# A reordered middle, reordered rotations, and a first output product in four pieces

## The chip, the cores and the metric

One core of a Trainium2 chip runs the whole program in one launch. The metric is the device time in microseconds. The kernel before took 2297.06, 2299.01 and 2300.14 us in three runs, median 2299.01.

## The reference

Two blocks in float32 on 1024 tokens of width 1024. The first is a mixer and a squared-ReLU MLP, the second an attention with compressed queries and keys (MLA):

```
h = rmsnorm(x, ln_mlp_g);  x = x + square(relu(h @ w_mlp_up)) @ w_mlp_down    # width 4096
h = x @ w_in_2;  x_q, x_kv, k_rope_raw, gate_a, u_pool, gate_b = split(h)
q  = rms_norm(x_q) @ w_uq          # 4 heads of 128 + 64 rotated
kv = rms_norm(x_kv) @ w_ukv        # keys and values, 4 heads of 128
s = (q_nope @ k_nope + rope(q_rope) @ rope(k_rope)) * scale, causal;  o = softmax(s) @ v
y = concat(o * silu(gate_a), pool_branch(u_pool) * silu(gate_b)) @ w_out_2
out = layer_norm(alpha * x + y)
```

## The kernel before

All large products are made in three passes of TensorE from operands that are split into a high and a low part (hi x hi, hi x lo, lo x hi). ScalarE copies the high part, VectorE (activations) or GpSimd (weights) subtracts it for the low part.

**The MLP's steps.** Two-by-two block products are made by Winograd's seven products P1 to P7. Steps 0 to 15 multiply up, steps 16 to 31 down, steps 32 to 40 (the strip) are the second block's input projection. The list RUN holds (step, product) in the order of TensorE; in steps 1 to 31 it is P1 P5 P6 P2 P7 P3 P4. A run's number is its index: step 16 begins at run 112, step 17 at 119, step 18 at 126. run() of TensorE (L1558 to L1588) waits for the weight's low part (wt_ok, GpSimd L1196), for its banks (evicted) and for its operand's low part (t_ok), and issues 12 matmuls (L1585). P1, P6, P7 and P4 of a step add up in one pair of banks, P5 and P3 in another, P2 has a third; after each run VectorE's event() adds the banks into xB (L2951), and the next run in those banks waits for it.

**Weights.** SP loads a step's weight blocks as wraw (load_pair, L915). GpSimd makes the sums S1 to S4 (L1152 to L1168); ScalarE's weight_hi (L2205) copies the high part of each weight at the turn W_TURN; GpSimd subtracts (L1196). After run 117's weight GpSimd also makes hsum, the last sums of the hidden blocks (L1180 to L1185).

**Split operands of the down steps.** 56 pieces j, one for each product of two steps, come from staged loads. ScalarE's split_hi(j) (L2275) stands at turn T_TURN[j] of its loop, behind that turn's weight_hi; VectorE's split_lo(j) (L2983) stands behind event(T_TURN[j]). T_TURN is 1 apart for j up to 6, then 2 apart: 117, 119, 121, 123 for j=7 to 10, and so on to 213 for j=55. Piece j is first used in step 16 + 2(j // 7), by the product P1, P5, P6, P2, P7, P3 or P4 as j % 7 is 0 to 6. So j=13 (turn 129) is used by run 132, j=20 (143) by run 146, and so on.

**SP in the middle.** At run 113 two loads of xB from x_d (1 MB each, L972 and L973) are issued, then staged loads; load_pair(st + 2) comes at the step's fourth run. Each waits in SP's one queue. event() of steps 16 and 17's P1 waits for those loads (x_in).

**Into the strip.** final_lo (L3033) splits the last results. The strip's operands T1 to T4 are differences of blocks of xB: t_sum (VectorE L3050, four operations each), t_his (ScalarE L2288), t_los (VectorE L3057). VectorE then evicts the strip by add_strip (L3121), ScalarE by copy_strip (L2295).

**Late strip and rotations.** ScalarE's root(xkv) (L1883, L1885), the reciprocal root of the compressed keys' mean square, stands ahead of step 40's copies. Then come the units uq (query heads) and ukv (keys, values): ScalarE copies each one's high part (q2st L2427, k L2436, V2h L2441), VectorE's low2 (L3242) the low part, which frees the bank. rope(r) (L3248 to L3250) rotates qr and kr with `turned`, which SP fills from kr and qr; rope_hi and rope_lo (L3258) split the result; the parts are parked in HBM and come back as q2S.

**The attention.** 32 items i, in pairs. TensorE issues logits2(i+2), turn2(i) (eight transposes, L1756), values2 (L1769). VectorE: least (L3299), normalise2 (L3307), turned_lo (L3312), gated (L3319). Behind them half_product (L1800) makes 16 units of the output product from actC, whose parts are split by branch_half (ScalarE) and low (VectorE L2528).

Of the kernel before, what the change touches and what calls it, by code (L numbers as in the profile page):

```python
# [18 lines left out]
ALU = mybir.AluOpType  # L19
# [195 lines left out]
RUN += [(st, p) for st in range(1, STEPS) for p in ("P1", "P5", "P6", "P2", "P7", "P3", "P4")]  # L215
# [12 lines left out]
for _st, _p in RUN:  # L228
    if WEIGHT[_p][0] == "S":
        SUM_NO[_st, _p] = len(SUM_NO) + 1  # L230
# [4 lines left out]
T_RING, STAGED = 10, 8  # L235

# [53 lines left out]
def split_turns():  # L290

    turn, room = [], []
    for j in range(N_SPLIT):
# [6 lines left out]
        turn.append(max(r, turn[-1] + (2 if j >= 7 else 1)) if turn else r + 2)  # L300
# [46 lines left out]
def build(nc, t):  # L347

    with ExitStack() as ctx:
# [395 lines left out]
        def product_bank(c):  # L745

            n = FIRST["out2"] + c
            col = (c // 2) % 2 * HALF
            return pair[n % 2][:, col:col + HALF]
# [68 lines left out]
        def _(sp):  # L818
# [148 lines left out]
            for at_run in range(7 * N_PAIR, N_ALL):  # L967
                if at_run == 7 * N_PAIR + 1:
# [4 lines left out]
                    sp.dma_start(xB[:, 1:4:2, :], x_d[:, 1:4:2, :]).then_inc(x_in, 16)  # L973
                st, p = RUN[at_run - 1]
# [3 lines left out]
                if at_run == START[st] + 3 and st + 2 < ALL_STEPS:  # L978
                    load_pair(st + 2)
# [79 lines left out]
        def _(pool):  # L1059
# [112 lines left out]

            def last_unit_sums():
# [13 lines left out]
            for i, (st, p) in enumerate(RUN):  # L1187
                if p in ("P1", "Q1"):
                    pool.wait_ge(pair_in[st % 2], 16 * (st // 2 + 1))
                if i + 1 < N_ALL and WEIGHT[RUN[i + 1][1]][0] == "S":  # L1190
                    weight_sum(i + 1)
                pool.wait_ge(wt_hi, i + 1)
# [40 lines left out]
        def _(pe):  # L1233
# [539 lines left out]

            pe.wait_ge(r_hi, 3)
# [3 lines left out]
            for i in range(N2 + 2):  # L1778
                if i + 2 < N2:
                    logits2(i + 2)  # L1780
                if i < N2:
                    turn2(i)
                if i >= 2:
                    values2((i - 2) // 2, i % 2)

            def half_product(j, half):
# [6 lines left out]
                if c == 1:  # L1793
                    pe.wait_ge(branch_ok, N2_GROUP)
                for k in range(NT):
                    if j == 0:
                        pe.wait_ge(lo_ok, base + 6 + half * NT + k + 1)
# [22 lines left out]
            for half in range(2):  # L1820
                half_product(0, half)
# [27 lines left out]
        def _(act):  # L1849
# [433 lines left out]
            def t_his(name):  # L2283

                c = ("T1", "T2", "T4", "T3").index(name)
                act.wait_ge(tsum_ok, T_SUMS + (16 if name == "T4" else 4 * c + 4))
# [20 lines left out]
            for at_run in range(2, N_RUN):  # L2307
# [5 lines left out]
                if at_run == 7:  # L2313
                    for p in ("P2", "P7", "P3", "P4"):
                        square_out(NO[0, p])
                late = START[N_PAIR + 1]
# [7 lines left out]
                for j in range(N_SPLIT):  # L2324
                    if T_TURN[j] == at_run:
# [36 lines left out]
            for i in range(START[STEPS + 1], N_ALL):  # L2362
# [31 lines left out]
                if i == NO[STEPS + 7, "P4"]:  # L2394
                    root(("stat", "xkv"), (squares_used, STAT_BASE["xq"] + 2), EPSV, rstd_kv[:, :])
                if i == NO[STEPS + 8, "P6"]:
# [7 lines left out]
            for r in range(2):  # L2404
                read_unit(n, n % 2, n // 2, qr[:, r, :], ACT.Copy)
                n += 1
                if r == 0:
                    act.wait_ge(lo_ok, base + 6)
# [14 lines left out]
            for h in range(4):  # L2423
# [7 lines left out]
                if h < 3:  # L2431
                    rope_hi(h)
# [12 lines left out]
            def branch_half(half, tiles):  # L2445
                if tiles[-1] > 3:
                    act.wait_ge(gb_moved, 32)
# [16 lines left out]
            for i in range(N2):  # L2464
# [3 lines left out]
                if i == N2 - 2:  # L2468
                    branch_half(0, range(3))
# [1124 lines left out]
```

## Time and profile before

| | |
|---|---|
| profiled execution, its span | 2299.54 us, 2297.7 us |
| TensorE (PE) busy | 2235.4 us, 97% |
| VectorE (DVE) busy | 1694.5 us, 74% |
| GpSimd (POOL) busy | 1195.4 us, 52% |
| ScalarE (ACT) busy | 837.3 us, 36% |
| TensorE's mean granted clock, as a share of full speed | 0.995 |

The matmuls of a row overlap: a run's 12 follow each other every 0.227 us, though each one's own time is 0.39. A bracket at a row's end is the engine's idle time before it and what released it.

### The profile page before, as it was taken

The numbers are of one execution on the slowest core, as the hardware profiler recorded it, in microseconds if no ns is written. First come the engines' busy times: TensorE is split into PE (matmuls) and PEld (weight loads), VectorE is DVE, ScalarE is ACT, GpSimd is POOL, SyncE is SP. The second block draws the span as 40 slices with busy tenths as digits, with TensorE's granted clock in tenths as the row PEclk, the third lists the DMA queues.
The fourth block names the chain that finished last, engine by engine and source line by source line (L and its number), as shares of the span: only waits on it lengthen the run. The fifth ranks groups of instructions, "written<-read, shape, count | busy, mean of one in ns | idle before, by whom it ended". The sixth has DMA issues, their size and how long they took to land. (4 is left out here: it accounts for less than half of the span.)

```text
span 2297.7 us, 29211 instructions
## 1 busy us (share of the span) xinstructions
PE 2235.4 (97%) x10722; PEld 1849.6 (80%) x10722; DVE 1694.5 (74%) x2037; ACT 837.3 (36%) x1165; POOL 1195.4 (52%) x895
## 2 busy tenths in 40 slices
PE   7999999999999999999999999899999999999998
PEld 5678888888888899787878888788888777778886
DVE  7899999986778354446587766677777866578777
ACT  4312243123334256213343333444343434344423
POOL 4136553333323266334478988998886678400140
PEclk9999999999999999999999999999999999999999
DMA  4121123633332422444234445654442212441231
GB/s 155 37 83 64 64 92 106 169 138 113 108 128 92 129 66 65 156 146 165 83 135 153 151 171 189 256 193 156 147 156 101 70 37 92 131 152 49 65 110 73
DMA packets 93733, 272.50 MB, mean 119 GB/s; under 512 B 8800, under 2 KB 25320, under 8 KB 87080
## 3 DMA queue, kind: packets, MB, share of 16 engines
q1 hardware_dynamic: 76544, 206.86, 26.8%
q10 hardware_dynamic: 17064, 63.99, 7.9%
q8 instruction: 77, 1.26, 0.2%
q14 instruction: 48, 0.39, 0.1%
HBM read 186.13 MB, written 83.90 MB: 118 GB/s over the span
## 5 line engine op out<-in xcount | busy, mean ns | idle before, releaser
L1247 PE MATMUL pair<-actA,w_hi 128*128 128x512 f32 x2016 | 624.5, 391 | 2.1 <-issue 2.1
L1247 PEld LDWEIGHTS pair<-actA,w_hi 128*128 128x128 f32 x2016 | 377.5, 188 | 81.4 <-ACT sq L1938 2.9
L1247 PE MATMUL pair<-actA,w_lo 128*128 128x512 f32 x1008 | 393.1, 390 | 0.0
L1066 POOL TENSOR_TENSOR pad<-pad 128x1 f32<-128x1 f32 x93 | 24.7, 266 | 585.3 <-PE pair L1247 506.4
L1585 PE MATMUL pair<-tring,wsp 128*128 128x512 f32 x1344 | 307.4, 391 | 8.1 <-issue 7.1
L1585 PEld LDWEIGHTS pair<-tring,wsp 128*128 128x128 f32 x1344 | 253.2, 189 | 62.2 <-issue 9.0
L1196 POOL TENSOR_TENSOR wsp<-wraw,wsp 128x512 fp32r<-128x512 f32 x124 | 188.8, 1523 | 75.5 <-ACT wsp L2205 75.1
L1247 PEld LDWEIGHTS pair<-actA,w_lo 128*128 128x128 f32 x1008 | 189.5, 188 | 39.8
L1070 POOL TENSOR_TENSOR w_lo<-raw,w_hi 128x1024 fp32r<-128x1024 f32 (+1 forms) x93 | 209.1, 2248 | 7.5
L1585 PE MATMUL pair<-tsp,wsp 128*128 128x512 f32 x768 | 184.2, 391 | 4.4 <-DVE tsp L2910 2.1
L2951 DVE TENSOR_TENSOR xB<-pair,xB 128x1024 f32<-128x1024 f32 x112 | 136.3, 1219 | 70.3 <-PE pair L1585 70.1
L2638 DVE MAX8 top<-pen 128x8 f32<-128x384 f32 (+5 forms) x192 | 171.7, 894 | 6.4
L1585 PEld LDWEIGHTS pair<-tsp,wsp 128*128 128x128 f32 x768 | 143.5, 188 | 37.5 <-DVE tsp L2910 4.3
L2640 DVE MATCH_REPLACE8 pen<-top,pen 128x384 f32<-128x384 f32 (+5 forms) x192 | 168.2, 876 | 0.0
L1585 PE MATMUL pair<-bsp,wsp 128*128 128x512 f32 x576 | 138.4, 389 | 0.0
L2205 ACT CAST wsp<-wraw 128x512 fp32r<-128x512 f32 x124 | 77.0, 621 | 160.4 <-PE pair L1585 140.2
L1196 POOL TENSOR_TENSOR wsp<-wsum_a,wsp 128x512 fp32r<-128x512 f32 x80 | 127.7, 1596 | 9.0 <-ACT wsp L2205 9.0
L1585 PEld LDWEIGHTS pair<-bsp,wsp 128*128 128x128 f32 x576 | 108.1, 188 | 22.5
L1922 ACT ACTIVATE stage<-pair 128x1024 f32<-128x1024 f32 x40 | 41.0, 1026 | 228.1 <-PE pair L1247 228.1
L1610 PE MATMUL pair<-bin,wsp 128*128 128x512 f32 x456 | 109.2, 393 | 3.4 <-ACT u L2295 2.1
L2983 DVE TENSOR_TENSOR tring<-staged,tring 128x1024 fp32r<-128x1024 f32 x56 | 97.7, 1744 | 13.9 <-ACT tring L2275 13.9
L1610 PEld LDWEIGHTS pair<-bin,wsp 128*128 128x128 f32 x456 | 86.6, 190 | 22.2 <-issue 4.2
(454 smaller groups left out, 4530.2 us busy)
## 6 DMA issues: line engine op xcount, KB each, us to landing
wraw<-w_pair SPq DMA_DIRECT2D x41, 1024.0 KB, 6.0
raw<-w_in SPq DMA_DIRECT2D x62, 512.0 KB, 3.5
staged<-hid_d SPq DMA_DIRECT2D x56, 512.0 KB, 3.3
proj<-stage ACTq DMA_DIRECT2D x40, 512.0 KB, 2.6
hid_d<-hsum SPq DMA_DIRECT2D x16, 1024.0 KB, 5.0
gates<-proj ACTq DMA_DIRECT2D x18, 512.0 KB, 5.2
raw<-w_out SPq DMA_DIRECT2D x16, 512.0 KB, 3.5
hid_d<-hid SPq DMA_DIRECT2D x16, 512.0 KB, 2.8
```

Source lines behind the costliest of these rows:

```text
L1066: nc.gpsimd.tensor_tensor(pad[:, 0:1], pad[:, 1:2], pad[:, 1:2], ALU.add)
L1070: nc.gpsimd.tensor_tensor(w_lo[:, par, 0:w], raw[:, par, 0:w], w_hi[:, par, 0:w].bitcast(F32), ALU.subtract).then_inc(w_split, 1)
L1196: nc.gpsimd.tensor_tensor(dst[:, 1, :], src, dst[:, 0, :].bitcast(F32), ALU.subtract).then_inc(wt_ok, 1)
L1247: last = nc.tensor.matmul(pair[par][:, cols], w[:, slot, wk], x[:, cols], start=(k == 0 and i == 0), stop=(k == kt - 1 and i == 2))
L1585: mm = nc.tensor.matmul(out, w[:, wp, wk], x[:, xp, k, :], start=(fresh and k == 0 and m == 0), stop=(k == ks - 1 and m == 2), skip_group_ ...
L1610: mm = nc.tensor.matmul(out, w[:, wp, wk], x(xp, k), start=(first and k == 0 and m == 0), stop=(last and k == 3 and m == 2), skip_group_ch ...
L1922: nc.scalar.activation(dst, pair[par][:, :], func).then_inc(unit_out[par], 1)
L2205: nc.scalar.copy(wsp[W_SLOT[i]][:, 0, :], src).then_inc(wt_hi, 1)
L2638: V.max(top8[:, :], sc).then_inc(topk, 1)
L2640: V.match_replace(sc, top8[:, :], sc, PICKED).then_inc(topk, 1)
L2951: V.tensor_tensor(acc, src.rearrange("p (s n) -> p s n", n=HALF), acc, ALU.add).then_inc(evicted, 1)
L2983: V.tensor_tensor(dst[:, 1, :, :].rearrange("p k n -> p (k n)"), staged[:, j % STAGED, :], dst[:, 0, :, :].rearrange("p k n -> p (k n)").b ...
```

## The change

Five places, each on several engines.

- Step 17's order becomes P1 P5 P2 P6 P7 P3 P4. T_TURN[8] becomes 121 (it was 119), T_TURN[9] 122 (121), and each later j's turn is one run later. ScalarE issues split_hi(6) and (7) at run 115, ahead of that turn's other copies. SP issues load_pair(18) right behind the two loads of xB and then waits for these before the staged loads.
- T3's four sums move from VectorE to GpSimd (third_sum, ahead of the weight of the first run of step 33). On VectorE T1's sums stand behind final_lo and T2's ahead of t_los("T1").
- root(xkv) moves behind step 40's P6 copy; norm2 of xkv moves behind the low parts of xq. The rotations' operations are spread otherwise between the units, and the load of cs waits for no low part any more.
- The first unit of the output product, half_product(0, 0), becomes first_product: four pieces of six matmuls at items 30 and 31, between the last two values and after the loop. It writes to the bank of item 30's logits. Its inputs are split one tile an item (VectorE, items 25 to 30) or two (ScalarE, items 24, 26, 28, 30).
- The product's second unit waits for the gated group 15 and the fourth for group 16, where the second waited for 16.

```diff
 RUN = [(0, p) for p in ("P1", "P5", "P2", "P6", "P3", "P7", "P4")]
-RUN += [(st, p) for st in range(1, STEPS) for p in ("P1", "P5", "P6", "P2", "P7", "P3", "P4")]
+RUN += [(st, p) for st in range(1, N_PAIR + 1) for p in ("P1", "P5", "P6", "P2", "P7", "P3", "P4")]
+RUN += [(N_PAIR + 1, p) for p in ("P1", "P5", "P2", "P6", "P7", "P3", "P4")]
+RUN += [(st, p) for st in range(N_PAIR + 2, STEPS) for p in ("P1", "P5", "P6", "P2", "P7", "P3", "P4")]
...
     if WEIGHT[_p][0] == "S":
-        SUM_NO[_st, _p] = len(SUM_NO) + 1
+        SUM_NO[_st, _p] = len(SUM_NO) + 1 + 4 * (NO[_st, _p] > NO[STEPS + 1, "P5"])
...
 T_RING, STAGED = 10, 8
+FIRST_HALF = [0, 4, 1, 5, 2, 6, 3, 7]
...
         room.append(r)
-        turn.append(max(r, turn[-1] + (2 if j >= 7 else 1)) if turn else r + 2)
+        if j == 8:
+            r = max(r, NO[N_PAIR + 1, "P2"])
+        turn.append(max(r, turn[-1] + (2 if j >= 7 and j != 9 else 1)) if turn else r + 2)
...
             col = (c // 2) % 2 * HALF
+            if c == 0:
+                return mpair(("qk", 1, N2 - 2))[:, 0:HALF]
...
                     sp.dma_start(xB[:, 1:4:2, :], x_d[:, 1:4:2, :]).then_inc(x_in, 16)
+                    load_pair(N_PAIR + 2)
+                    sp.wait_ge(x_in, 16 * (NT + 6))
...
                 st = RUN[at_run][0]
-                if at_run == START[st] + 3 and st + 2 < ALL_STEPS:
+                if at_run == START[st] + 3 and N_PAIR < st < ALL_STEPS - 2:
...
+            def third_sum():
+
+                pool.wait_ge(tsum_ok, T_SUMS + 4)
+                pool.wait_ge(lo_ok, 4 * NT + 4)
+                for k in range(4):
+                    nc.gpsimd.tensor_tensor(xB[:, k, HALF:S], xB[:, 4 + k, HALF:S], xB[:, k, HALF:S],
+                                            ALU.subtract).then_inc(summed, 1)
+                sums[0] += 4
...
                     weight_sum(i + 1)
+                if i == START[STEPS + 1]:
+                    third_sum()
...
+            def first_product(part):
+                n, out = FIRST["out2"], product_bank(0)
+                whi, wlo = kept(0)
+                if part == 0:
+                    pe.wait_ge(w_split, n + 1)
+                    wait_done(pe, ("qk", 1, N2 - 2))
+                for s in (2 * part, 2 * part + 1):
+                    k = FIRST_HALF[s]
+                    pe.wait_ge(lo_ok, base + 6 + s + 1)
+                    wk, xh, xl = slice(k * P, (k + 1) * P), actC[:, 0, k, 0, :], actC[:, 0, k, 1, :]
+                    for i, (w, x) in enumerate(((whi, xh), (whi, xl), (wlo, xh))):
+                        mm = nc.tensor.matmul(out, w[:, wk], x, start=(s == 0 and i == 0),
+                                              stop=(s == NT - 1 and i == 2))
+                if part == 3:
+                    mm.then_inc(unit_mm, 1)
...
                     logits2(i + 2)
+                if N2 - 2 <= i <= N2:
+                    first_product(i - N2 + 2)
...
                     values2((i - 2) // 2, i % 2)
+            first_product(3)
...
                 if c == 1:
+                    pe.wait_ge(branch_ok, N2_GROUP - 1)
+                if c == 3:
...
                     if j == 0:
-                        pe.wait_ge(lo_ok, base + 6 + half * NT + k + 1)
+                        pe.wait_ge(lo_ok, base + 6 + NT + k + 1)
...
             for half in range(2):
-                half_product(0, half)
+                if half:
+                    half_product(0, half)
...
-                c = ("T1", "T2", "T4", "T3").index(name)
-                act.wait_ge(tsum_ok, T_SUMS + (16 if name == "T4" else 4 * c + 4))
+                if name == "T3":
+                    act.wait_ge(summed, SUM_NO[STEPS + 1, "P5"] + 4)
+                else:
+                    act.wait_ge(tsum_ok, T_SUMS + 4 * ("T1", "T2", "T4").index(name) + 4)
...
                         square_out(NO[0, p])
+                if at_run == NO[N_PAIR, "P2"]:
+                    split_hi(6)
+                    split_hi(7)
...
                 for j in range(N_SPLIT):
-                    if T_TURN[j] == at_run:
+                    if T_TURN[j] == at_run and j not in (6, 7):
...
                     root(("stat", "xq"), (squares_used, STAT_BASE["xq"] + 1), EPSV, rstd_q[:, :])
-                if i == NO[STEPS + 7, "P4"]:
+                if i == NO[STEPS + 8, "P6"]:
                     root(("stat", "xkv"), (squares_used, STAT_BASE["xq"] + 2), EPSV, rstd_kv[:, :])
-                if i == NO[STEPS + 8, "P6"]:
...
                 if r == 0:
-                    act.wait_ge(lo_ok, base + 6)
...
                     park_q2(h - 1)
-                if h < 3:
-                    rope_hi(h)
+                if h != 1:
+                    rope_hi(max(h - 1, 0))
...
             def branch_half(half, tiles):
-                if tiles[-1] > 3:
-                    act.wait_ge(gb_moved, 32)
+                act.wait_ge(gb_moved, 32)
...
                 turned_hi(i)
-                if i == N2 - 2:
-                    branch_half(0, range(3))
-            branch_half(0, range(3, NT))
+                if i % 2 == 0 and i >= N2 - 8:
+                    s = i - N2 + 8
+                    branch_half(0, FIRST_HALF[s:s + 2])
...
-                c = ("T1", "T2", "T4", "T3").index(name)
+                c = ("T1", "T2", "T4").index(name)
...
                     b11, b12_, b21, b22 = xB[:, k, 0:HALF], xB[:, k, HALF:S], xB[:, 4 + k, 0:HALF], xB[:, 4 + k, HALF:S]
-                    x, y = {"T1": (b12_, b11), "T2": (b22, b11), "T3": (b22, b12_), "T4": (b21, t2f[:, k, :])}[name]
+                    x, y = {"T1": (b12_, b11), "T2": (b22, b11), "T4": (b21, t2f[:, k, :])}[name]
...
                     final_lo(("P5", "P6", "P7", "P3").index(p))
-                if st == STEPS - 1 and p == "P7":
-                    t_sum("T1", (0, 1))
-            t_sum("T1", (2, 3))
+            t_sum("T1", (0, 1))
...
                 final_lo(c)
+            t_sum("T1", (2, 3))
+            t_sum("T2")
             t_los("T1")
-            t_sum("T2")
...
             t_los("T2")
-            t_sum("T3")
...
             norm2([(g, xq[:, g, :]) for g in range(1, 4)], "q_norm_2", rstd_q)
-            dve.wait_ge(rstd_ok, 13)
-            norm2([(g, xkv[:, g, :]) for g in range(2)], "kv_norm_2", rstd_kv)
...
                 low(base + g, xq_lo[:, g, :], xq[:, g, :], xq_hi[:, g, :])
+            dve.wait_ge(rstd_ok, 13)
+            norm2([(g, xkv[:, g, :]) for g in range(2)], "kv_norm_2", rstd_kv)
...
                 low2(n, q2_hi, h + 1, q2st[:, h % 2, 1, :], q2st[:, h % 2, 0, :]).then_inc(unit_out[n % 2], 1)
-                if h < 2:
-                    rope(h)
-                for k in ((), (), (0,), (1, 2))[h]:
-                    rope_lo(k)
+                if h == 0:
+                    rope_lo(0)
+                elif h == 1:
+                    rope(0)
+                elif h == 2:
+                    rope(1)
+                    rope_lo(1)
...
                 low2(n, kv_hi, h + 1, k2[:, 1, h, :], k2[:, 0, h, :]).then_inc(unit_out[n % 2], 1)
+                if h == 0:
+                    rope_lo(2)
...
+
+            def first_low(s):
+                j = FIRST_HALF[s]
+                low(base + s, actC[:, 0, j, 1, :], branch(j, 0), actC[:, 0, j, 0, :])
...
                     gated(i // 2 - 2)
-                if i == N2 - 2:
-                    low_half(0, range(3))
-            low_half(0, range(3, 6))
+                if N2 - 7 <= i < N2 - 1:
+                    first_low(i - N2 + 7)
             gated(N2_GROUP - 2)
-            low_half(0, range(6, NT))
+            first_low(6)
+            first_low(7)
```

## Rows read from the trace of the kernel before

**Rows 1.** The page: busy time of TensorE and its weight loads.
```profile
PE 2235.4 (97%) x10722; PEld 1849.6 (80%) x10722; DVE 1694.5 (74%) x2037; ACT 837.3 (36%) x1165; POOL 1195.4 (52%) x895
```

**Rows 2.** Waits of TensorE from 1440 us on: total, times, longest, all in us.
```profile
PE pair L1247 <- DVE q2st L3242: 2.6, 2, 1.4
...
PE pair L1756 <- DVE PTl L3312: 2.3, 2, 1.2
...
PE pair L1247 <- DVE k L3242: 1.8, 1, 1.8
PE pair L1610 <- DVE bin L3033: 1.3, 1, 1.3
PE pair L1769 <- DVE PTl L3312: 0.9, 1, 0.9
```

**Rows 3.** Timeline of TensorE, 1486 to 1503: start, length, instruction, count.
```profile
1494.37 7.28 PE L1585 MATMUL pair<-tring,wsp 128*128 128x512 f32 x24 [6.87 <-issue]
1501.84 1.39 PE L1585 MATMUL pair<-tring,wsp 128*128 128x512 f32 x5 [0.19 <-issue]
```

**Rows 4.** Timeline of VectorE, 1466 to 1503.
```profile
1490.16 1.84 DVE L2983 TENSOR_TENSOR tring<-staged,tring 128x1024 fp32r<-128x1024 f32 x1 [9.56 <-ACT tring L2275]
1491.93 2.34 DVE L2951 TENSOR_TENSOR xB<-pair,xB 128x1024 f32<-128x1024 f32 x2
```

**Rows 5.** Timeline of ScalarE, 1466 to 1503.
```profile
1489.09 1.04 ACT L2275 CAST tring<-staged 128x1024 fp32r<-128x1024 f32 x1
```

**Rows 6.** Timeline of GpSimd, 1466 to 1503.
```profile
1490.88 2.25 POOL L1196 TENSOR_TENSOR wsp<-wraw,wsp 128x512 fp32r<-128x512 f32 x1
1495.86 1.28 POOL L1152 TENSOR_TENSOR wsum_a<-wraw 128x512 f32<-128x512 f32 x1 [2.73 <-DMA wraw<-w_pair]
```

**Rows 7.** Timelines of VectorE in the down steps, 1557 to 1565 and 1580 to 1585.
```profile
1560.39 1.24 DVE L2983 TENSOR_TENSOR tring<-staged,tring 128x1024 fp32r<-128x1024 f32 x1
...
1581.01 1.23 DVE L2951 TENSOR_TENSOR xB<-pair,xB 128x1024 f32<-128x1024 f32 x1 [1.24 <-PE pair L1585]
1582.15 1.93 DVE L2983 TENSOR_TENSOR tring<-staged,tring 128x1024 fp32r<-128x1024 f32 x1
```

**Rows 8.** Timeline of TensorE, 1580 to 1585: two runs without a stall.
```profile
1579.67 5.60 PE L1585 MATMUL pair<-tring,wsp 128*128 128x512 f32 x24
```

**Rows 9.** Timeline of GpSimd, 1578.5 to 1585.
```profile
1581.71 1.29 POOL L1196 TENSOR_TENSOR wsp<-wsum_c,wsp 128x512 fp32r<-128x512 f32 x1 [0.66 <-ACT wsp L2205]
```

**Rows 10.** Timelines of VectorE, GpSimd and TensorE into the strip, 1775 to 1825.
```profile
1789.13 2.49 DVE L3050 TENSOR_TENSOR t2f<-xB 128x512 f32<-128x512 f32 x4
...
1795.91 6.48 DVE L3057 TENSOR_TENSOR bin<-t2f,bin 128x512 fp32r<-128x512 f32 x4 [0.60 <-ACT bin L2288]
1802.31 6.87 DVE L3050 TENSOR_TENSOR xB<-xB 128x512 f32<-128x512 f32 x4
1809.88 8.50 DVE L3057 TENSOR_TENSOR tA<-xB,tA 128x512 fp32r<-128x512 f32 x8 [0.69 <-ACT tA L2288]
...
1792.71 1.45 POOL L1196 TENSOR_TENSOR wsp<-wraw,wsp 128x512 fp32r<-128x512 f32 x1 [11.64 <-ACT wsp L2205]
...
1819.08 3.00 PE L1610 MATMUL pair<-tA,wsp 128*128 128x512 f32 x12 [2.04 <-issue]
```

**Rows 11.** Timeline of TensorE late in the strip, 1947 to 2046.
```profile
1955.12 7.27 PE L1610 MATMUL pair<-bin,wsp 128*128 128x512 f32 x24 [2.09 <-ACT u L2295]
```

**Rows 12.** Stretches: length, busy PE, PEld, DVE, ACT, POOL (instructions), PE clock, DMA, GB/s.
```profile
1468.00:1487.50 19.50, 19.32 (x84) 15.69 (x84) 11.51 (x10) 5.31 (x8) 19.42 (x14) 1.00 0.46 171
...
1955.07:1958.48 3.41, 3.36 (x8) 2.71 (x9) 2.96 (x2) 1.42 (x3) 2.92 (x2) 0.50 0.01 2
```

**Rows 13.** Stretches of the key units, with the same columns.
```profile
2020.00:2026.00 6.00, 5.22 (x23) 4.35 (x24) 2.90 (x3) 1.06 (x2) 0.00 (x0) 1.00 1.01 351
```

**Rows 14.** Timeline of TensorE, 2020 to 2050: the first logits.
```profile
2037.73 0.47 PE L1741 MATMUL pair<-k,q2S 128*128 128x512 f32 x1 [0.28 <-issue]
```

**Rows 15.** Timeline of VectorE in the last items, 2155 to 2205.
```profile
2165.09 1.40 DVE L3307 TENSOR_SCALAR L<-L,tiny 128x1024 f32<-128x1024 f32 x1
```

## Prediction

> **What bounds the kernel now.** First the page's line of busy times: TensorE works 2235.4 of 2297.7 us [rows 1], so the end is set by PE, and a reordering can win only PE's idle time, 62.3 us in all, or time in which PE ran at its lower clock. Then PE's waits over the last 850 us and the stretches around each: a 6.87 us stall in the middle [rows 3], 1.3 where the last down step passes into the strip, 2.09 late in the strip [rows 11], 2.6 and 1.8 in the rotations, 2.3 and 0.9 at the end of the attention [rows 2]. These are the places that the change touches. The reader is to ask at each: which instruction ended the wait, what stood ahead of it in its own queue, and what is next to be late. Last, the steady rhythm of the down steps [rows 7, 8], which loses nothing now and whose order the change also shifts.
>
> The profiled execution took 2299.54 us (span 2297.7 and 1.84 around it). The sum is made against that; the median of the timed runs is 2299.01, 0.5 less. A measurement here can tell about 0.2% (4.6 us) from no change.
>
> **A1, the middle.** Run 121 (step 17's third) starts at 1494.37 after 6.87 of idling [rows 3]. It needed two evictions of DVE, which ended at 1494.27; in DVE's queue they stood behind split_lo(7), which sat from 1480.6 to 1490.16 for ScalarE's split_hi(7) [rows 4]; that copy began at 1489.09 [rows 5], behind five weight copies that wait for GpSimd's sums. The change issues split_hi(6) and (7) ahead of those copies, so this block goes, and run 121 becomes a P2, whose bank pair is another. Runs 121 and 122 then end at 1487.34 + 24 x 0.227 = 1492.8. (A run is 12 matmuls at 0.227, or 2.72; a row of 24 matmuls shows 5.60 with the last one's own length in it [rows 8].)
>
> What is late next? Run 123 (P7) now follows P6 directly in one bank pair and needs P6's eviction. On DVE that eviction stands behind split_lo(8), moved from turn 119 to 121. split_lo(8) waits for split_hi(8), and in ScalarE's queue that stands at turn 121 behind weight_hi(128), the copy of step 18's S2. GpSimd makes that sum only after the weight splits of step 17, of which the last ends at 1493.13 [rows 6]. Before, GpSimd then idled 2.73 for wraw(18) [rows 6]; the load is moved forward, right behind the two xB reloads, so this idling goes. Sum S1, a split and sum S2 at 1.28 each (as the first sum there) end at 1497.0; split_hi's 1.04 [rows 5] and the copy ahead of it, half as wide, some 0.6: 1498.7; split_lo 1.9 [rows 4]: 1500.6; eviction 1.17 (2.34 for two): 1501.8. Run 123 starts at about 1501.9; before, it started at 1501.84 [rows 3]. The stall is moved from in front of run 121 to in front of run 123. Behind the stall of 6.87 the next 24 matmuls took 7.28 for 5.60 [rows 3, 8], as behind the one late in the strip, where the granted clock was 0.50, the 1.2 GHz level, for 3.4 us [rows 12]. That comes again, now behind run 123: +1.7 at most. I take **+1.5**, bounds 0 and +3.5 (the second adds staged loads that now wait for x). If split_lo(8) holds nothing up, only P6's eviction itself lies between the runs, about 1.4: run 123 at 1494.2, or **-7.6**.
>
> **A2, the turn of every later split.** From j=9 each split_lo comes one run later. For most it is needed 4 to 9 runs after its turn. But the split of the P4 quarter in each even step (j=13, 20, ... 55, seven of them) had 3 runs and now has 2. j=20 runs alone, 1.24, at 1560.39 [rows 7]; with one run more it lands where the odd steps have a split now, as j=24: PE's run releases the eviction at 1581.01 (0.20 after its end, by the starts of its matmuls), the split takes 1582.15 to 1584.08 [rows 7], 1.93 instead of 1.24 because GpSimd's weight split of 1581.71 [rows 9] overlaps it. So it ends 3.07 + 0.20 = 3.27 after the run's end, and PE needs it 2.72 after: 0.55 late, 0.15 for the semaphore, some 0.08 to restart: 0.78 x 7 = **+5.3** (bounds: 0 if it runs in 1.24, ending 2.58 after; +7 at 1.0 each, if GpSimd begins its 1.29 just ahead of it).
>
> **B, into the strip.** T1's first sums no longer stand ahead of final_lo(4), so the 1.30 wait goes [rows 2]. T3's four sums, 6.87 on DVE, go to GpSimd, idle for 11.64 there [rows 10]. But GpSimd's four sums now meet DVE's: four DVE operations of this shape took 2.49 while GpSimd was idle, and 6.48 beside it [rows 10]. T2's sums and T1's low parts, 2.49 each, now cost up to 6.5 each, the GpSimd weight work starts a microsecond later, and T2's low parts end near 1812 rather than 1802.4. T4's low parts end at 1820 to 1822 against 1818.4, and P4 waits for the addition behind them, as before at 1819.08 [rows 10]. I take **+2.5**, bounds -1.7 (no clash) and +3.8.
>
> The row shows DVE at 1.62 an operation beside GpSimd. The Trainium skill (SBUF — State Buffer, "SBUF: two separate sides") says that whichever of the two starts first holds the shared ports for its whole instruction, and Perfetto Trace Analysis ("Optimizing Scalar/DVE Operations") that work moved between these two engines might not help. The trace agrees as to the blocking. By the rule in full GpSimd's four sums would hold the ports 4 x 1.28 = 5.1 us where DVE's held them 2.5, and B would be about +2.6, an estimate.
>
> **C, the end of the strip and the rotations.** root(xkv), two activations with a table load each, moves on ScalarE behind (40,P6); the strip copy it held up comes in time. It cost 2.09 of stall, and the 24 matmuls behind it took 7.27 for 5.60 [rows 8, 11] at the low clock [rows 12]: with 0.15 to restart -3.9. Of the rotations' stalls, the first (1.2, on the landing of turned) stays, since its whole chain moves along; the second (1.4) and that of the third key unit (1.8) go [rows 2], and one of some 0.5 is new (by the lengths of the same instructions in their new order), at the second key unit behind rope(1) and its low part. That would be -6.5. But logits2(0) waits for q2S, issued into a stretch in which the DMA engines are full [rows 13] and whose first transfer moves only with the 3.9 and not with the two stalls. So PE arrives earlier and waits there: before it waited 0.28 [rows 14]. **-3.3**, bounds -2.2 (a stall at the value units halves the clock for a while, as here at 1955: 1.7) and -6.5 (q2S in time).
>
> **D, the last items.** At the end of the items PE lost 2.3 and 0.9 to the transposed low parts [rows 2]. The first product's 24 matmuls come in between in four pieces of 6 (1.36 us each) and no longer behind: the 3.2 of idling go, with 0.15 of restart at each of the three, -3.65 at best. In exchange DVE gets one more low part (0.6) in each of six items, and beside GpSimd's split of w_out a DVE operation of 0.75 elsewhere took 1.40 [rows 15]; one such can push the next transposes by 0.6 and, with a low part in between, up to 1.75. The bank, GpSimd's later splits and the loads are free in time. **-2.5**, bounds -1.9 and -3.65.
>
> **Sum**: 1.5 + 5.3 + 2.5 - 3.3 - 2.5 = +3.5: 2303.0 by the profiled execution, **2302.5** against the median: no change that can be told, a shade slower. Its own range is 2298 to 2307.
>
> **Rivals.**
> 1. *The middle's stall goes.* For it: the only thing that holds P6's eviction is a split that is first used six runs on, and GpSimd could be ahead of my sum, if wraw(18) is there by 1488 and its operations run at 1.28. Against it: GpSimd is busy 19.42 of the 19.50 us up to the stall [rows 12] and cannot start step 18 before 1493.1. A1 is then -7.6: 3.5 - 9.1 = -5.6, 2293.4.
> 2. *Slower: DVE and GpSimd take turns at full price.* Place: the seven shifted splits, the strip's start and the last six items; price: A2 +6.5, B +3.8, D -1.9, so 1.5 + 6.5 + 3.8 - 3.3 - 1.9 = +6.6, 2305.6. It decides where each DVE operation begins after GpSimd's, not before. For it: the odd steps' 1.93 repeats all the way through; against: off the path it costs nothing, as in every odd step now.
> 3. *The shifted splits cost nothing.* If DVE begins ahead of GpSimd each time (as at 1560.39), A2 is 0: -1.8, 2297.2. Against it: it is the odd steps' own pattern that the even ones take over.
> 4. *The change does not fill the tail*, D = 0, as the pieces wait for their low parts: +6, 2305; small.
>
> **How the numbers follow.** Forecast 0.45, rival 1 0.20, rival 2 0.18, rival 3 0.12, rival 4 0.05. Faster by over 0.2% (below 2294.4): most of rival 1 and a part of rival 3 with rival 1's gain, 0.22. Slower by over 0.2% (above 2303.6): rivals 2 and 4 and a quarter of the forecast, 0.34. Between: 0.44. The range takes in rival 1 with a larger C below (2291) and rival 2 with A1's far end above (2309).
>
> **What would show it.** A1: run 121 without a stall, and an idle of 8 to 9 us ahead of run 123 with split_lo(8) at about 1499 on DVE. A2: seven PE waits of 0.5 to 0.9 on DVE's tring, 38.1 us apart. B: DVE's T2 sums at 1.6 to 1.7 each. C: no wait on u at 1953, 24 matmuls in 5.44, and a longer wait ahead of the first logits. D: transposes of the last items that follow without a gap. The prediction fails if run 123 starts by 1495, if DVE's splits stay at 1.24 in those seven places, or if the wait at the first logits doesn't appear.

## Result and profile after

The changed kernel takes 2322.06 us in the median of four runs (2317.85 to 2323.35) against 2299.57 for the kernel before in four runs: a ratio of 1.0088, 95% interval [1.0072, 1.0104], slower by 0.9%. I had forecast 2302.5 and a range up to 2309. The profiled execution's span is 2320.2 against 2297.7. TensorE works hardly longer (2235.4 before, [rows 1]); the page of the changed kernel begins with its busy time, share and count:

```profile
PE 2241.8 (97%) x10722; PEld 1852.1 (80%) x10722; DVE 1704.1 (73%) x2033; ACT 838.2 (36%) x1165; POOL 1198.6 (52%) x899
```

Cut at the same matmuls in both traces, the difference stands where the prediction's terms are (us, from the starts of TensorE's first matmuls in the two profiled executions):

| stretch | before | after | differs | forecast |
|---|---|---|---|---|
| run 119 to run 130 (A1) | 39.07 | 45.61 | +6.5 | +1.5 |
| run 130 to the strip (A2) | 255.68 | 260.47 | +4.8 | +5.3 |
| the strip's first 16 products (B) | 47.99 | 51.27 | +3.3 | +2.5 |
| the rest of the strip (C, first part) | 145.75 | 141.82 | -3.9 | -3.9 |
| last input unit to the first logits (C, rest) | 67.34 | 69.41 | +2.1 | +0.6 |
| first logits to item 24 | 104.96 | 104.86 | -0.1 | 0 |
| item 24 to the end (D) | 154.99 | 165.12 | +10.1 | -2.5 |

TensorE's waits of the changed kernel from 1440 us on, with total, times and longest, answer to [rows 2]:

```profile
PE pair L1605 <- issue: 13.6, 1, 13.6
PE pair L1847 <- DVE xB L3411: 9.1, 1, 9.1
PE pair L1267 <- DVE q2st L3284: 5.4, 1, 5.4
PE pair L1605 <- DVE tring L3027: 4.0, 7, 0.7
PE pair L1630 <- DVE bin L3101: 2.6, 2, 2.2
PE pair L1776 <- DVE PTl L3359: 2.1, 3, 1.8
```

The larger waits of before at the places of the change are gone, and larger ones stand in their stead. The first two are the surprise. In the middle, the timelines of the changed kernel's TensorE, VectorE and GpSimd answer to [rows 3, 4, 6]:

```profile
1506.32 26.54 PE L1605 MATMUL pair<-tring,wsp 128*128 128x512 f32 x108 [13.63 <-issue]
...
1498.35 6.73 DVE L3027 TENSOR_TENSOR tring<-staged,tring 128x1024 fp32r<-128x1024 f32 x1 [6.71 <-ACT tring L2317]
1505.00 1.21 DVE L2995 TENSOR_TENSOR xB<-pair,xB 128x1024 f32<-128x1024 f32 x1
...
1497.84 1.27 POOL L1216 TENSOR_TENSOR wsp<-wsum_b,wsp 128x512 fp32r<-128x512 f32 x1
1499.06 1.27 POOL L1170 TENSOR_TENSOR wsum_a<-wraw 128x512 f32<-128x512 f32 x1
1500.29 1.27 POOL L1216 TENSOR_TENSOR wsp<-wraw,wsp 128x512 fp32r<-128x512 f32 x1
1501.51 1.27 POOL L1177 TENSOR_TENSOR wsum_c<-wraw,wsum_b 128x512 f32<-128x512 f32 x1
1502.72 1.27 POOL L1216 TENSOR_TENSOR wsp<-wsum_a,wsp 128x512 fp32r<-128x512 f32 x1
```

Run 123 waits, as forecast, for the eviction behind split_lo(8), and split_lo(8) starts at 1498.35 where I had 1498.7. But it takes 6.73 us for work of 1.2. It ends at 1505.08, 1.09 behind the last of five GpSimd operations in a row, four of which began after it and none of which was lengthened. In the changed kernel's end, VectorE, GpSimd and TensorE:

```profile
2206.95 6.39 DVE L2572 TENSOR_TENSOR actC<-u,actC 128x512 fp32r<-128x512 f32 x4 [0.76 <-ACT actC L1934]
2213.26 7.61 DVE L2572 TENSOR_TENSOR actC<-gb,actC 128x512 fp32r<-128x512 f32 x4
2220.91 1.41 DVE L3411 SCALAR_TENSOR_TENSOR xB<-xB,pair 128x512 f32<-128x512 f32 x2
...
2207.26 1.29 POOL L1247 CAST w_kept<-raw 128x1024 fp32r<-128x1024 f32 x1 [22.14 <-PE pair L1805]
2208.62 2.73 POOL L1249 TENSOR_TENSOR w_kept<-raw,w_kept 128x1024 fp32r<-128x1024 f32 x1
...
2221.65 2.07 PE L1847 MATMUL pair<-xB,cst 128*128 128x512 f32 x2 [9.10 <-DVE xB L3411]
```

The first product now ends as the values end, so GpSimd's third weight split (released by TensorE's L1805 at 2207.26) begins just when VectorE begins the eight low parts of half 1. These take 14.0 us where the kernel before took 5.0, and the operation that the first mean waits for (L3411) stands behind them.

### The profile page after: what moved, and what is told of

Same layout as the page of the kernel before. It is cut to its first block and busy times, and to the rows that moved or that the text cites. A ratio compares the mean times of both kernels' runs of the same rounds, so it can differ in the third digit from the quotient of the medians.

```text
span 2320.2 us, 29212 instructions
## 1 busy us (share of the span) xinstructions
PE 2241.8 (97%) x10722; PEld 1852.1 (80%) x10722; DVE 1704.1 (73%) x2033; ACT 838.2 (36%) x1165; POOL 1198.6 (52%) x899
## 5 line engine op out<-in xcount | busy, mean ns | idle before, releaser
L1605 PEld LDWEIGHTS pair<-bsp,wsp 128*128 128x128 f32 x576 | 108.1, 188 | 22.5
```

Source lines behind the costliest of these rows:

```text
L1605: mm = nc.tensor.matmul(out, w[:, wp, wk], x[:, xp, k, :], start=(fresh and k == 0 and m == 0), stop=(k == ks - 1 and m == 2), skip_group_ ...
```

## Experiments

Ratios are to the kernel before on the same chip, with their 95% intervals. Stretches are those of the table, each from one profiled execution. Runs of one kernel spread by 3 to 20 us, so a difference of 2 us between two experiments is read from the stretches and not from the whole times.

**1. The first product's result taken out first.**

```diff
             dve.wait_ge(branch_ok, N2_GROUP)
-            low_half(1, range(NT))
...
+            move(0)
+            low_half(1, range(NT))
             dve.wait_ge(lo_ok, base + 2 * NT)
...
-                move(c)
+                if half:
+                    move(c)
```


> The changed kernel with one edit at the end: VectorE takes the first product's result out (move(0)) ahead of the eight low parts of half 1, not behind them. Theory (the 9.10 us wait ahead of the first mean is VectorE's queue: move(0) stands behind eight low parts that take 14.0 us instead of 5.0, because GpSimd's weight splits, which the earlier first product releases earlier, now fall on them): the low parts still take 12 to 14 us, but the wait ahead of the first mean falls under 1 us and the run is 8 to 9.5 us faster than the changed kernel, about 2313. Rival (the pieces of the first product or the borrowed bank hold the mean up): the wait stays at 9 and the time at 2322.

Measured: 2310.90 us, 1.0055 [1.0037, 1.0073]. The stretch from item 24 on fell from 165.12 to 153.90. The low parts still took 13.2 us, but nothing waits for them; of the end's waits two of 1.8 and 0.4 are left, beside one of 0.7 that the kernel before has too. The theory holds; it gave two us more than the wait, as the matmuls behind it no longer run slowly (in the changed kernel 25 of them had taken 7.62, at a granted clock of 0.72, where 25 at 0.227 take 5.7).

**2. GpSimd's third split waits for the low parts.**

```diff
                 if j == 2:
                     pool.wait_ge(unit_mm, FIRST["out2"] + 1)
-                if j == 6:
                     pool.wait_ge(lo_ok, 4 * NT + 10 + 2 * NT)
```


> The changed kernel with one edit at the end: GpSimd's third weight split of the output product waits until VectorE's sixteen low parts are done. Theory (shared SBUF access of VectorE and GpSimd): the eight low parts of half 1 fall from 14.0 to about 5.0 us, the wait ahead of the first mean from 9.10 to under 1.5; the third unit's weights come some 3 us late, so 5 to 8 us faster than the changed kernel, 2314 to 2317. Rival (the low parts are slow for a reason of their own, as their place in SBUF or the copies beside them): they stay at 12 to 14 us and nothing is won.

Measured: 2313.57 us, 1.0068 [1.005, 1.0085]. VectorE in this kernel:

```profile
2204.50 2.50 DVE L2571 TENSOR_TENSOR actC<-u,actC 128x512 fp32r<-128x512 f32 x4 [0.76 <-ACT actC L1933]
2206.91 2.49 DVE L2571 TENSOR_TENSOR actC<-gb,actC 128x512 fp32r<-128x512 f32 x4
```

The same eight operations take 5.0 us when GpSimd holds still: it is GpSimd's work that makes them 14. The 9.10 went and 1.77 for the later weights came. The theory holds. The run is 8.5 us faster than the changed kernel, half a us more than expected. It also showed that the middle has two outcomes. Its code there is that of the changed kernel, and its VectorE:

```profile
1499.64 1.85 DVE L3026 TENSOR_TENSOR tring<-staged,tring 128x1024 fp32r<-128x1024 f32 x1 [7.02 <-ACT tring L2316]
1501.42 1.21 DVE L2994 TENSOR_TENSOR xB<-pair,xB 128x1024 f32<-128x1024 f32 x1
```

Here GpSimd let it in after one operation, and the stall is 8.77. Run 123 starts at 1502.73, 19.8 behind run 119; forecast were 1501.9 and 20.0. In four of the five profiles with this middle (the changed kernel, 1, 5 and 6) it was 13.63 or 13.64.

**3. GpSimd pauses in the middle until split_lo(8) is done.**

```diff
+                if i == NO[N_PAIR + 2, "P6"]:
+                    pool.wait_ge(t_ok, 16 + 9)
                 if i + 1 < N_ALL and WEIGHT[RUN[i + 1][1]][0] == "S":
```


> The changed kernel with one edit in the middle: GpSimd makes the sum S2's successors of step 18 (from the weight of its P6 on) only when split_lo(8) is done. Theory (split_lo(8) took 6.73 us instead of 1.2 to 1.9 because five GpSimd operations in a row went ahead of it): it falls to 1.2 to 2.6 us, run 123 starts 4 to 5.5 us earlier, at about 1502, the stall ahead of it is about 9 us, and the run is 4 to 5 us faster than the changed kernel, about 2317.5. Rival (the length of split_lo(8) has another cause, as the staged loads that land beside it): 6 to 7 us as before, run 123 at 1506.

Measured: 2315.42 us, 1.0073 [1.0055, 1.009]. VectorE and GpSimd of this kernel:

```profile
1497.82 1.23 DVE L3029 TENSOR_TENSOR tring<-staged,tring 128x1024 fp32r<-128x1024 f32 x1 [6.89 <-ACT tring L2319]
...
1499.13 1.27 POOL L1218 TENSOR_TENSOR wsp<-wsum_b,wsp 128x512 fp32r<-128x512 f32 x1 [1.77 <-DVE tring L3029]
```

The theory holds: split_lo(8) takes 1.23 and the stall falls to 8.14, so 5.5 us of the 13.63 are GpSimd's operations that went ahead. The rest is the order, in which split_lo(8) still waits 6.89 for its high part.

**4. The turns of before.**

```diff
-        if j == 8:
-            r = max(r, NO[N_PAIR + 1, "P2"])
-        turn.append(max(r, turn[-1] + (2 if j >= 7 and j != 9 else 1)) if turn else r + 2)
+        turn.append(max(r, turn[-1] + (2 if j >= 7 else 1)) if turn else r + 2)
```


> The changed kernel with the turns of the splits (T_TURN) as they were before; step 17's order and all else stay. Theory: split_lo(8) no longer stands ahead of run 122's eviction, so run 123 starts at 1495 to 1498 instead of 1506.3, and the six waits of 0.54 in the even steps go: 11 to 15 us faster than the changed kernel, 2307 to 2311. Rival (it is GpSimd's unbroken work that holds VectorE's splits, wherever they stand): the six waits go (3.7 us), but split_lo(8), now ahead of run 120's eviction, is held to 1500 or later and the stall only moves: 3 to 6 us faster, 2316 to 2319.

Measured: 2316.49 us, 1.0075 [1.0056, 1.0094]. Run 130 to the strip takes 255.68, to the hundredth that of before: the later turns cost 4.8, as forecast. But run 123 starts at 1502.65 still. VectorE:

```profile
1494.87 1.89 DVE L3025 TENSOR_TENSOR tring<-staged,tring 128x1024 fp32r<-128x1024 f32 x1 [5.50 <-ACT tring L2315]
1496.68 2.34 DVE L2993 TENSOR_TENSOR xB<-pair,xB 128x1024 f32<-128x1024 f32 x2
1499.57 1.85 DVE L3025 TENSOR_TENSOR tring<-staged,tring 128x1024 fp32r<-128x1024 f32 x1 [0.55 <-ACT tring L2315]
1501.34 1.21 DVE L2993 TENSOR_TENSOR xB<-pair,xB 128x1024 f32<-128x1024 f32 x1
```

The time is the rival's, and so is the stall that only moves, but not the place: split_lo(8) is through by 1496.8, and now split_lo(9) at its turn 121 stands ahead of run 122's eviction, behind a high part that waits for the same sum of GpSimd. The 11 to 15 us of the theory come only when every split leaves the way (experiment 7).

**5. T3's sums back on VectorE**, on top of experiment 1.

```diff
             t_sum("T1", (2, 3))
             t_sum("T2")
             t_los("T1")
             t_sum("T4")
             t_los("T2")
+            t_sum("T3")
             t_los("T3")
...
-                if i == START[STEPS + 1]:
-                    third_sum()
```


> The first experiment's kernel (the first product's result taken out ahead of half 1's low parts) with T3's four sums back on VectorE, behind t_los(T2) as before; T1's and T2's sums stay where the change put them. Theory (GpSimd's four sums cost more in VectorE's other sums, which go from 0.6 to 1.7 each, than they take from it): T2's sums fall from 6.9 to about 2.5 us, the wait of 2.2 us at T2's low parts and the 3 us of slow matmuls behind it go; a wait of 0 to 2 at T4's low parts comes back; 2 to 5 us faster than the first experiment. Rival (VectorE's 2.4 to 6.9 us saved count): T4's low parts come late again, the stretch is as long or 1 to 2 us longer.

Measured: 2310.98 us, 1.0056 [1.0039, 1.0072]; the strip's first products take 51.52 against 51.22 in experiment 1. The rival holds. T2's sums fell to 2.50, and the wait only moved, to T4's low parts (TensorE of this kernel):

```profile
1830.83 4.35 PE L1619 MATMUL pair<-tA,wsp 128*128 128x512 f32 x11 [5.24 <-issue]
```

So T3's place alone gives nothing back. With the order of T1's and T2's sums undone as well the stretch is 47.99, 49.59 and 49.56 (experiments 9 to 11). T3 on GpSimd with the old order of the sums was not run.

**6. The rotations' order of before**, on top of experiment 1.

```diff
-                if h == 0:
-                    rope_lo(0)
-                elif h == 1:
-                    rope(0)
-                elif h == 2:
-                    rope(1)
-                    rope_lo(1)
+                if h < 2:
+                    rope(h)
+                for k in ((), (), (0,), (1, 2))[h]:
+                    rope_lo(k)
```
(and rope_hi in ScalarE's loop)

> The first experiment's kernel with the rotations' order on VectorE and ScalarE as before; root(xkv) stays behind step 40's P6 and the load of cs still waits for no low part. Theory (in the changed order ScalarE's copy of the third query head waits for a parked one to land in HBM, 6.5 us of idling, and its successor follows late): the 4 to 5 us wait at the second key unit becomes waits of 1.2, 1.4 and 1.8, and the stretch from the first query unit to the first logits falls by 1 to 3 us against the first experiment. Rival (the stretch is set by the DMA engines, whichever order): the first logits come as late, within 0.5 us.

Measured: 2308.94 us, 1.0044 [1.0028, 1.0061]. The last input unit to the first logits: 63.95 against 67.74, and against 67.34 in the kernel before. The waits of 1.2 and 1.4 did not come back, only that of 1.73: 3.8 us, more than expected, and the rival fails.

**7. The middle's splits behind the evictions**, on top of experiment 1: split_lo(8), (9), (10) at turns 122, 123, 124, the later ones at those of before.

```diff
+                if at_run in (119, 120, 121):
+                    split_hi(at_run - 111)
                 late = START[N_PAIR + 1]
...
-                    load_pair(N_PAIR + 2)
-                    sp.wait_ge(x_in, 16 * (NT + 6))
```


> The first experiment's kernel with the middle ordered so that no split stands ahead of an eviction that step 17 needs: split_lo(8), (9), (10) behind runs 122, 123, 124 and every later one at its turn of before, their high parts on ScalarE ahead of the weight copies at runs 119 to 121, and load_pair(18) back behind the staged loads. Theory (run 123 is held by P6's eviction alone once the splits are out of VectorE's way): the stall ahead of run 123 falls from 9 to 14 us to 1.3 to 3, the slow clock behind it goes, the six waits of 0.54 go: 12 to 17 us faster than the first experiment, 2294 to 2299. Rival (GpSimd's unbroken work holds VectorE wherever the splits stand): waits of together 6 to 10 us come up in the runs 124 to 131 instead, and 4 to 8 us are won.

Measured: 2297.75 us, 0.9995 [0.9985, 1.0005], 13.2 faster than experiment 1, in the theory's range. The stall ahead of run 123 is 1.36, but a new one of 4.75 came five runs later (TensorE, VectorE of this kernel):

```profile
1494.05 13.88 PE L1603 MATMUL pair<-tring,wsp 128*128 128x512 f32 x60 [1.36 <-issue]
1512.69 7.53 PE L1603 MATMUL pair<-tring,wsp 128*128 128x512 f32 x25 [4.75 <-POOL wsp L1214]
...
1510.12 1.33 DVE L3027 TENSOR_TENSOR tring<-staged,tring 128x1024 fp32r<-128x1024 f32 x1 [5.96 <-ACT tring L2315]
1511.37 2.34 DVE L2995 TENSOR_TENSOR xB<-pair,xB 128x1024 f32<-128x1024 f32 x2
```

The label says GpSimd; but run 128's weight was split by 1504.2 in this trace, and the eviction of run 126, behind split_lo(11), ended at 1512.6. Experiment 9 tests this.

**8. All parts together**: 7, 5, 6 and 1.

> All of these together: step 17's new order with its splits out of the way, T3's sums on VectorE, the rotations' old order, root(xkv) moved, and the first product in four pieces with its result taken out ahead of half 1's low parts. If the parts add: the first experiment less 12 to 17, less 2 to 5, less 1 to 3, so 2287 to 2296, and faster than the kernel before by 3 to 11 us. If the sum is set by other waits in its stead (the rivals of the three): 2299 to 2304.

Measured: 2294.86 us, 0.9982 [0.9973, 0.9992]: 2287 to 2296 holds, though 5 gave nothing.

**9. The high parts of splits 8 to 13 ahead of the weight copies, the load early, the strip as before.**

```diff
-                if at_run in (119, 120, 121):
+                if at_run in range(119, 125):
                     split_hi(at_run - 111)
...
+                    load_pair(N_PAIR + 2)
...
-            t_sum("T1", (2, 3))
-            t_sum("T2")
             t_los("T1")
+            t_sum("T2")
```
(T1's first two sums too stand where they stood before)

> The kernel of all parts together with three edits: the high parts of splits 8 to 13 all stand ahead of ScalarE's weight copies (runs 119 to 124), where 8 to 10 did; load_pair(18) stands right behind the two loads of xB again; and the way into the strip is as in the kernel before (T3 on VectorE, T2's sums behind T1's low parts). Theory (the 5 us wait that came up ahead of run 128 is split_lo(11), which waits for its high part behind a weight copy that waits for GpSimd, and holds run 126's eviction): it goes, and from the start of run 119 to that of run 130 it takes 31.5 to 34 us instead of 38.6; the strip's first five steps take 48.0 instead of 51.7; in all 2284 to 2288, 11 to 15 us faster than the kernel before. Rival (GpSimd itself is late with the weights of step 18, as the profile's label at that wait says): with the load earlier 2 to 3 us of the 5 go, 35.5 to 37 for the eleven runs, in all 2288 to 2291.

Measured: 2288.00 us, 0.9956 [0.9941, 0.9971]: faster than both kernels. From run 119 to run 130 it takes 31.54, the strip's first products 47.99, and no wait is left between run 123 and run 135 (TensorE):

```profile
1493.93 32.90 PE L1593 MATMUL pair<-tring,wsp 128*128 128x512 f32 x144 [1.36 <-issue]
1528.56 1.62 PE L1593 MATMUL pair<-tring,wsp 128*128 128x512 f32 x6 [1.72 <-issue]
```

The rival had 35.5 to 37 for the first. So it was VectorE's queue and not GpSimd's lateness, although the load came earlier in the same run: in experiment 7's trace the weight had been there 8.5 us before the wait ended. Run 130 to the strip takes 257.69, 2.0 more than before, with the 1.72 ahead of run 135 in it.

**10. The load of cs waits again**, on top of 9.

```diff
                 if r == 0:
+                    act.wait_ge(lo_ok, base + 6)
                     act.wait_ge(cs_gb0_moved, 32)
```


> The kernel of the run before this one with one edit: the load of cs waits for the sixth low part again, as in the kernel before. Theory (of the rotations the change's only gain is this earlier load: the first rotation no longer waits for it, nor the transfers that stood beside it): from the end of the strip's last units to the first logits it takes 67 to 67.5 us instead of 63.9, 3 to 3.5 us slower than the run before. Rival (the gain comes from the later normalisation of xkv or from what lies around it): 64 to 65, no difference that can be told.

Measured: 2292.51 us, 0.9981 [0.9964, 0.9998]. The last input unit to the first logits: 67.02 against 63.94. The theory holds by this stretch, and the waits of the rotations (2.6 in two, 1.8) are those of before again. By the whole times alone it could not be told: twelve runs from 2286 to 2303, and an interval that meets experiment 9's.

**11. The end as before**, on top of 9 without its pieces.

```diff
-                if N2 - 2 <= i <= N2:
-                    first_product(i - N2 + 2)
...
-            first_product(3)
...
             for half in range(2):
-                if half:
-                    half_product(0, half)
+                half_product(0, half)
```
(and the low parts, high parts and bank of the first product as before)

> The ninth experiment's kernel with the end of the attention and the first unit of the output product as in the kernel before (no pieces, no early low parts; half_product(0, 0) behind the values). Theory (with GpSimd's splits falling on VectorE's low parts the pieces win 3 us of waits and lose 1.5 to 2.2 at a transpose behind a slowed normalisation, so they are worth 1 us or less): from the 24th item on 154.5 to 155.5 us where the pieces took 153.6 to 156.1 in five profiles; the time within 1.5 us of 2288.0. Rival (the pieces are worth what I forecast, 2.5): 156.5 to 158, 2290.5.

Measured: 2288.08 us, 0.9959 [0.9943, 0.9975]; from item 24 on 154.99, to the hundredth that of the kernel before. With the pieces and the result taken out first it was 153.62 to 156.09 in seven profiles (1, 5 to 10), 154.24 in the mean. So the pieces are worth 0.8 by the profiles and nothing that can be told by the times; the theory holds.

## Why the prediction was wrong

- **The sum.** +3.5 forecast, 22.5 measured. Three terms were right in sign and within a microsecond (A2, B, the first part of C), and so was the place of the stall in A1; the error is D (12.6), A1 (5.0) and the rest of C (1.5).
- **D is the step that failed**: "The bank, GpSimd's later splits and the loads are free in time." Free they are, but that is the trouble. In the trace of the kernel before the first product ended at about 2196.4 and released GpSimd's third split at 2196.63, as VectorE's low parts ended (2197.2). VectorE and GpSimd of the kernel before:

```profile
2192.26 2.50 DVE L2528 TENSOR_TENSOR actC<-u,actC 128x512 fp32r<-128x512 f32 x4 [0.76 <-ACT actC L1892]
2194.68 2.49 DVE L2528 TENSOR_TENSOR actC<-gb,actC 128x512 fp32r<-128x512 f32 x4
...
2196.63 1.44 POOL L1227 CAST w_kept<-raw 128x1024 fp32r<-128x1024 f32 x1 [23.92 <-PE pair L1800]
```

There the split comes 4.4 us behind the start of the low parts, in the changed kernel 0.3 (2207.26 against 2206.95). Finishing the product earlier on TensorE released the split onto the low parts (experiment 2: 14.0 us beside it, 5.0 without), and the first mean waits behind them (experiment 1). I had priced the clash of the two engines only where the change adds work. The 3.2 us of waits went as forecast, 1.75 came back at one transpose, inside the bound that I gave. Where nothing waits for the low parts, too, the pieces are worth 0.8 and not 2.5 (experiment 11).
- **A1**: order and place right, the term "split_lo 1.9" mis-sized: 6.73 in four of five profiles. In the trace before every split of the down steps was let in after one operation of GpSimd's (2.31 at most; 1.84 and 1.93 in [rows 4, 7]); I took that for a rule. Rival 2 named the clash of the two engines, but in other places and by turns, and no row of before shows a split that five operations hold. With split_lo at 1.85 (experiment 2) the term is right and run 123 starts within 0.2 of the forecast, counted from run 119.
- **A2**: seven late splits at 0.78 (together 5.46; the prediction has 5.3). Measured 4.79 in six: each costs 0.8, so the price was right and the number of places one too many. At the seventh, j=55, GpSimd was idle, the split took 1.22 and run 216 did not wait. The row that answers to [rows 7], on VectorE and TensorE of the changed kernel:

```profile
1570.19 1.93 DVE L3027 TENSOR_TENSOR tring<-staged,tring 128x1024 fp32r<-128x1024 f32 x1
...
1572.26 2.97 PE L1605 MATMUL pair<-tring,wsp 128*128 128x512 f32 x12 [0.54 <-DVE tring L3027]
```

- **B**: right in size, for another reason. VectorE's operations went to 1.7 each as forecast, but experiment 5 shows that without this clash the strip is no shorter. Nor did TensorE wait longer: 2.20, 0.35 and 0.83 in these products, 3.4 together, against 1.30, 0.34 and 2.04 before, 3.7. The 3.3 is time at the low clock, which I had not counted: behind the stall of 2.20 the granted clock was 0.64 for 7.9 us, in which 21 matmuls took 7.93 where 4.9 is the usual; behind that of 2.04 before it was 1.00. VectorE, GpSimd and TensorE of the changed kernel, for [rows 10], and last the stretch behind the stall, with the columns of [rows 12]:

```profile
1798.02 6.92 DVE L3094 TENSOR_TENSOR t2f<-xB 128x512 f32<-128x512 f32 x4
...
1798.00 6.39 POOL L1187 TENSOR_TENSOR xB<-xB 128x512 f32<-128x512 f32 x4 [6.37 <-DVE xB L3094]
...
1820.38 1.25 PE L1630 MATMUL pair<-bin,wsp 128*128 128x512 f32 x3 [2.20 <-DVE bin L3101]
...
1821.90:1829.80 7.90, 7.77 (x22) 5.71 (x23) 7.13 (x11) 2.21 (x5) 3.15 (x2) 0.64 0.39 134
```

A part of this is luck. Experiments 9 and 10 have the same code in this stretch, with the same stall, but 47.99 and 49.59: the granted clock in the 3 us behind the stall was 1.00 in one and 0.61 in the other. TensorE of 9, then of 10:

```profile
1813.21 2.99 PE L1618 MATMUL pair<-tA,wsp 128*128 128x512 f32 x12 [2.01 <-issue]
...
1813.39 4.58 PE L1618 MATMUL pair<-tA,wsp 128*128 128x512 f32 x12 [2.01 <-issue]
```

- **C**: the moved root gave its 3.9. How the -3.3 follows from -3.9 and the waits is not worked out in the prediction. Two steps failed. "The first (1.2, on the landing of turned) stays, since its whole chain moves along": it went, because cs is loaded earlier; experiment 10 gives 3.1 us for that line. And the new wait "of some 0.5" was 5.39: the fourth head's low part stands behind rope(1), whose operations meet GpSimd, and rope_lo(1), which waits for a copy of ScalarE. TensorE and ScalarE of the changed kernel:

```profile
2028.99 0.77 PE L1267 MATMUL pair<-xkv_hi,w_hi 128*128 128x512 f32 x1 [5.39 <-DVE q2st L3284]
...
2017.52 1.01 ACT L2472 CAST q2st<-pair 128x1024 fp32r<-128x1024 f32 x1 [6.46 <-DMA q_d<-q2st]
...
2026.49 1.04 ACT L2466 CAST qr_hi<-qr 128x1024 fp32r<-128x1024 f32 x1 [3.52 <-DVE qr L3292]
```

The longer wait at the first logits did not appear, which the prediction itself names as a sign of failure, nor did it in experiment 6 with its 3.4 us shorter stretch. So up to there the full DMA engines were no floor.

The Trainium skill (SBUF — State Buffer, "SBUF: two separate sides") says that whichever of VectorE and GpSimd starts first holds the shared ports for the whole instruction. The trace agrees as to the blocking: 14.0 against 5.0 in experiment 2. It doesn't reach the 6.73 of A1, where four operations that began after VectorE's went ahead of it.

## What to carry to other kernels

When work is moved earlier on the engine that bounds, list what its end releases, and look what those engines' operations then fall on: here a weight split that had come late by luck cost 9 us. A stall behind an in-order queue moves to the next instruction that waits for the same slow producer; it goes only when everything that waits for it is taken out of the way (experiments 4, 7, 9), and the label of a wait can name the wrong engine of two. Change the parts one at a time: here the moved root, the earlier load of cs, and step 17's order with its splits out of the way are worth 11 us (experiments 9 and 11), where the whole cost 22.

## What I had not expected of the hardware

A split of VectorE's was held through five GpSimd operations in a row (6.72 to 6.74 us, in four profiles of five with the same code in the middle) and let in after one in the fifth (1.85). What decides it these runs don't show: GpSimd's first operation had begun 0.5 us earlier both times. The changed kernel's own times, 2317.85 against 2322.04 to 2323.35 for the other three, differ by about as much; whether for this reason isn't shown.

The granted clock behind a stall of 2.0 us was 1.00 in two kernels (before and experiment 9) and 0.61 and 0.62 in two others (10 and 11) with the same waits at the same place. A forecast to the microsecond has this in it, 1.6 us here.
